# Two-block transformer kernel: the modulation products end with the attention, and three chunks of the first expert get homes

## The reference

```python
for l in range(DEPTH):                                    # 2 layers
    mod   = (silu(c)     @ ada_w[l] + ada_b[l])           # "modulation": ada_w[l] is 1024 x 6144
    mod_c = (silu(c_ctx) @ ada_w[l] + ada_b[l])
    sh1, sc1, g1, sh2, sc2, g2 = split(mod, 6)
    hx = rms_norm(x, norm1_g[l]) * (1 + sc1) + sh1        # and hc likewise for the context
    px = hx @ w_in[l]                                     # projection
    # four mixers on parts of px: spatial gating, fourier, attention "c" (differential), attention "d" (neighbourhood)
    x = x + g1 * (rms_norm(y, per head) @ w_out[l])       # merge
    h = rms_norm(x, norm2_g[l]) * (1 + sc2) + sh2
    aff = softmax(h @ router_w[l])                        # 16 experts, each takes its 32 best tokens of a stream
    x = x + g2 * sum over experts of gate * (silu(xe @ wg[e]) * (xe @ wu[e])) @ wd[e]
```

## Time and profile before

| | |
|---|---|
| median of 3 runs | 2338.39 us |
| lowest and highest run | 2334.14 and 2344.38 us |
| profiled execution, span from first to last instruction | 2346.5 us |
| PE busy, share of the span | 2140.5 us, 91% |
| DMA | 660.95 MB, mean 282 GB/s |
| layer 0 up to the first product of expert 0 | 0 to 323 us |
| layer 0's experts | 323 to 780 us |

### The profile page before, as it was taken

How to read it: one execution, slowest core, us unless ns; L and a number is a source line. 1 busy time by engine, 2 the same in 40 slices (tenths; PEclk the granted TensorE clock), 3 DMA queues, 4 the chain that set the end, 5 groups by cost and what they waited for, 6 DMA issues and landing times.

```text
span 2346.5 us, 33361 instructions
## 1 busy us (share of the span) xinstructions
PE 2140.5 (91%) x14368; PEld 1483.4 (63%) x14368; DVE 1132.2 (48%) x1775; ACT 844.9 (36%) x1258; POOL 44.2 (2%) x76
## 2 busy tenths in 40 slices
PE   9999999989898999966565789999999999999998
PEld 5866743423232777533232348888988888888887
DVE  5646531212121777310010138668877677568765
ACT  4436321111111556200000025445655455456544
POOL 0022000000000011000000000000000000000000
PEclk9999999999999999988888899999999999999999
DMA  8375679999999553999999994454554544364442
GB/s 347 120 318 246 257 310 425 427 427 428 428 427 426 201 224 140 377 427 426 428 427 427 426 407 182 149 210 171 189 190 159 195 180 180 135 234 180 157 172 88
DMA packets 66978, 660.95 MB, mean 282 GB/s; under 512 B 7504, under 2 KB 10576, under 8 KB 21136
## 3 DMA queue, kind: packets, MB, share of 16 engines
q1 hardware_dynamic: 66832, 658.83, 69.3%
HBM read 657.76 MB, written 1.05 MB: 281 GB/s over the span
## 4 chain that ended last, share of the span: by engine, by line
PE 69%; DMA 24%; DVE 3%; ACT 2%; issue 1%; SPq 0%; DVEq 0%; ACTq 0%
PE ps L967 21%; PE ps L1460 11%; PE ps L968 10%; DMA ring_top<-in_exp_up 9%; DMA ring_top<-in_exp_down 5%; PE ps L937 5%; PE ps L938 5%; PE ps L939 5%; DMA ring_top<-in_exp_gate 4%; DMA ring<-in_exp_up 3%; PE ps L986 2%; DMA ring<-in_exp_down 1%; DMA ring<-in_ada_w 1%; PE ps L1154 1%; PE ps L1453 1%; PE ps L1417 1%
## 5 line engine op out<-in xcount | busy, mean ns | idle before, releaser
L967 PE MATMUL ps<-h_buf_r,ring_r 128*128 128x512 f32 x800 | 283.8, 399 | 1.5 <-DVE h_buf_r L759 1.5
L1460 PE MATMUL ps<-ring,arena 128*32 128x256 f32 (+1 forms) x1632 | 215.0, 514 | 67.3 <-DMA ring<-in_exp_up 38.0
L2787 DVE TENSOR_TENSOR h_buf<-h_buf,ps 128x512 f32<-128x512 f32 (+1 forms) x32 | 17.8, 555 | 490.0 <-PE ps L1460 478.1
L968 PE MATMUL ps<-h_buf_r,ring_r 128*128 128x256 f32 x800 | 224.7, 281 | 0.0
L967 PE MATMUL ps<-h_buf_r,ring_top_r 128*128 128x512 f32 x608 | 217.4, 402 | 2.9 <-DVE h_buf_r L759 2.9
L1460 PE MATMUL ps<-ring_top,arena 128*32 128x256 f32 (+1 forms) x1328 | 164.2, 512 | 59.5 <-DMA ring_top<-in_exp_up 29.0
L1460 PEld LDWEIGHTS ps<-ring,arena 128*32 128x32 f32 (+1 forms) x1632 | 80.1, 132 | 199.0 <-issue 109.5
L485 DVE TENSOR_TENSOR ring_r<-ring,ring_r 128x2048 fp32r<-128x2048 f32 (+4 forms) x92 | 177.7, 1967 | 50.6 <-ACT ring_r L477 50.5
L967 PEld LDWEIGHTS ps<-h_buf_r,ring_r 128*128 128x128 f32 x800 | 150.3, 188 | 39.2 <-issue 1.9
L968 PE MATMUL ps<-h_buf_r,ring_top_r 128*128 128x256 f32 x608 | 171.4, 282 | 0.0
L1460 PEld LDWEIGHTS ps<-ring_top,arena 128*32 128x32 f32 (+1 forms) x1328 | 61.9, 133 | 159.1 <-issue 84.6
(11 more groups left out here) (390 smaller groups left out, 4144.7 us busy)
## 6 DMA issues: line engine op xcount, KB each, us to landing
ring<-in_exp_gate SPq DMA_DIRECT2D x35, 2048.0 KB, 28.2
ring<-in_exp_down SPq DMA_DIRECT2D x35, 2048.0 KB, 30.5
ring<-in_exp_up SPq DMA_DIRECT2D x34, 2048.0 KB, 30.2
ring_top<-in_exp_gate SPq DMA_DIRECT2D x29, 2048.0 KB, 29.1
ring<-in_ffn_w SPq DMA_DIRECT2D x50, 1024.0 KB, 6.9
ring_top<-in_exp_up SPq DMA_DIRECT2D x24, 2048.0 KB, 30.7
ring_top<-in_exp_down SPq DMA_DIRECT2D x24, 2048.0 KB, 28.3
ring_top<-in_ffn_w SPq DMA_DIRECT2D x38, 1024.0 KB, 6.9
```

Of the source, the lines that this page charges most:

```text
L967: release(pe.matmul(ps[:, bank, :], w[0][:, lo:lo + P], both, start=start, stop=False, skip_group_check=True))
L968: return pe.matmul(ps[:, bank, 0:N], w[1][:, lo:lo + P], both[:, 0:N], start=False, stop=stop, skip_group_check=True)
L1460: mm = pe.matmul(out, stationary, slot(c)[:, at:at + width], start=start, stop=stop)
```

## The change

Steps 1 and 2 of the modulation move into the projection: a pair of chunks behind each of the first four `w_in` chunks. Step 3 takes step 1's place ahead of the fourier mixer, steps 4 and 5 take the places of 3 and 4 among the units of attention d, and the block ahead of attention d and the four pieces in the route go away; in the route, products of zeros stand in their place. SP's list follows this order, so `w_in` and `ada_w` chunks alternate. At the start, the second half of step 0 is mixed with two products of the projection's second pair. The first expert's chunks c1, c2 and c3 get homes in `arena` (c2 had one already), the home of the modulation chunk goes, and a table of the experts (`aff_bc`) moves to make room. The squares for the second norm keep four tiles in turn instead of eight, since c3's home lies where the other four were. The core of the diff:

```diff
         HOMES = {
+            ("experts", 0, 1): [part(8192, 10240), part(14336, 16384)],
             ("experts", 0, 2): [part(10240, 14336)],
-            ("ada", 5, 3): [part(8192, 10240), part(14336, 16384)],
+            ("experts", 0, 3): [part(2048, 4096), part(6144, 8192)],
...
             if l == 0:
                 stream(("ada", 0), *[PLAIN] * 4)
-            stream(("w_in", l), HALVED, HALVED, HALVED, (2, SLOT), (1, KT * GROUP))
-            if l == 0:
-                for step in range(1, 5):
+                for c in range(4):
+                    stream(("w_in", 0, c), w_in_chunks[c])
+                    stream(("ada_pair", 1 + c // 2, c % 2), PLAIN, PLAIN)
+                stream(("w_in", 0, 4), w_in_chunks[4])
+                for step in range(3, 6):
                     stream(("ada", step), *[PLAIN] * 4)
...
+                        if l == 0 and (e, c) == (1, 0):
+                            sp.wait_ge(sem("d_pv"), len(units(0)))
+                            load_expert_home(0, 1)
+                            load_expert_home(0, 2)
+                            sp.wait_ge(sem("y_turned"), KT)
+                            load_expert_home(0, 3, (0,))
+                        if l == 0 and (e, c) == (1, 2):
+                            sp.wait_ge(sem("mix_out"), KT)
+                            load_expert_home(0, 3, (1,))
...
+                if i == 1 and k >= 4:
+                    act.wait_ge(sem("mix_square_added"), k - 3)
+                act.activation(square_of(i, k)[:, 0:width], x_res[:, k, 0:width], ACT.Square).then_inc(sem("norm_squares"), 1)
...
                     first_pair(0, range(0, 4))
-                    for c in range(2):
-                        first_ada_products(1, c)
-                    first_pair(1, range(0, 2))
+                    first_ada_products(1, 0)
+                    first_pair(1, (0,))
+                    first_ada_products(1, 1)
+                    first_pair(1, (1,))
                     first_ada_turn(1)
...
                     owed[0] += 1
+                    ada_products(1, (0, 1))
...
+                        if l == 0 and c in (1, 2, 3):
+                            ada_products(1 + c // 2, (2, 3) if c % 2 else (0, 1))
+                    elif l == 0 and t == 0 and c in (2, 4):
+                        ada_turn(c // 2)
...
                     pe.wait_ge(sem("c_out"), 4)
-                    ada_products(2)
...
-                        ada_products(3 + i // 4, (i % 4,))
+                        ada_products(4 + i // 4, (i % 4,))
...
                 if l == 0:
-                    ada_products(5, (0,))
+                    stay_busy(3, 8)
...
-                    ada_products(5, (1,))
+                    stay_busy(3, 6)
...
-                if l == 0:
-                    ada_products(5, (2,))
-                else:
-                    stay_busy(3, 2)
+                stay_busy(3, 2)
...
                 if l == 0:
-                    ada_products(1)
+                    ada_products(3)
```

More of the change, by code:

```diff
@@ L406, in build, with w_in, ada_chunk @@
             stream(("ple", l), HALVED, HALVED)
+        def w_in(l, c):
+            return chunk_at["w_in", l, c]
+        def ada_chunk(step, i):
+            return chunk_at["ada_pair", step, i // 2] + i % 2 if step in (1, 2) else chunk_at["ada", step] + i
         def expert_chunk(l, e):
@@ L572, in load_expert_home, with ada @@
                           P * SLOT * (2 * (EXPERTS * l + e) + which % 2), pieces)
[L574 to L578, removed]
-                    else:
[L580 to L584, removed]
+            def ada(step, pieces=range(4)):
+                for i in pieces:
+                    load(ada_chunk(step, i), "ada_w", SLOT)
             def ffn(i):
@@ L702, in squares, with square_of @@
                 part(2560, 4608).rearrange("p (k t) -> p k t", k=KT)
+        def square_of(i, k):
+            if i == 1:
+                return part(0, 2048).rearrange("p (k t) -> p k t", k=4)[:, k and 1 + (k - 1) % 3, :]
+            return squares(i)[:, k, :]
         def norm_pe(pe, release, i):
@@ L978, in ada_products @@
                     pe.wait_ge(sem("ada_mod"), step + 1)
[L979 to L987, removed]
+                for i in pieces:
+                    n = ada_chunk(step, i)
+                    chunk(n)
+                    for k in (2 * i, 2 * i + 1):
+                        for j in range(4):
+                            at = 2048 * (k % 2) + 512 * j
+                            mm = pe.matmul(ps[32 * j:32 * j + 32, 7, :], cond[:, k, :], slot(n)[:, at:at + 512],
+                                           start=k == 0, stop=k == KT - 1)
                             release(mm)
-                    if k % 2:
-                        mm.then_inc(weights_used, 1)
+                    mm.then_inc(weights_used, 1)
             def first_ada_products(half, c):
-                n = chunk_at["ada", 0] + 2 * half + c
+                n = ada_chunk(0, 2 * half + c)
                 if half == c == 0:
@@ L1029, in job_product @@
                     c, t, lo, width, _ = jobs[j]
-                    w = halves(base + c)
+                    w = halves(w_in(l, c))
                     own = slice(P * t, P * t + P)
@@ L1358, in token_means @@
                     own, out = slice(P * t, P * t + P), ps[:, 7, 64 + t:65 + t]
[L1359 to L1360 removed]
+                    release(pe.matmul(out, square_of(i, 0)[:, own], mean_col[:, :], start=True, stop=False))
+                    mm = pe.matmul(out, square_of(i, KT - 1)[:, own], mean_col[:, :], start=False, stop=True)
                 mm.then_inc(sem("norm_mean"), 1)
@@ L1503, in experts @@
                                 mm.then_inc(weights_used, 1)
-                            if l == e == which == 0 and k == 3:
-                                ada_turn(5)
                             if (which, k) != (1, KT - 1):
```

170 lines of the change are left out of this document (83 added, 87 removed).

## The result

The changed kernel takes 2345.3 us (median of 20 runs, 2342.5 to 2354.8) against 2341.5 us of the kernel before (20 runs): a ratio of 1.0026, with a 95% interval of 1.0017 to 1.0035, or +4 to +8 us. It is slower by less than the 0.5% that was set as the bound for "same"; 2343 us and "same" were forecast. The 2343 was reckoned from the 2338.4 us of three runs; what it says of the change is +4.6 us. The two medians differ by +3.9, and the ratio, which is not that of the medians, stands for +6 us.

A forecast was written before the change was run, and what follows sets the result against it. PE's progress to expert 0's chunk c4 was taken to start an unbroken DMA stream of 85 expert chunks. Terms 14.1 + 1.3 − 1.4 − 6.6 − 2.8 = +4.6 on 2338.4 gave 2343 us, range 2331 to 2355.

The forecast's parts named there:

- The homes at nothing: Layer 0's experts: homes for the first expert's c1 to c3 leave the start of the expert load stream unchanged, 0 us.
- The rival of two chunks ahead: Layer 0's experts: added homes shorten the load stream by 2 × 4.9 us, to 2333 us; chance 0.09.
- Projection, +14.1 + 1.3 − 1.4 = +14.0: Projection: two modulation steps add 14.1 us, their two turns 1.3, and a covered weight wait at the start saves 1.4.
- Attention d, −6.6: Attention d: without the block of step 2, the first value product starts 6.6 us earlier.
- The route with the turn, −2.8: Layer 0's route: four step 5 pieces replaced by zeros, and its turn inside expert 0 gone, save 2.8 us.
- Sum, +4.6: All terms up to PE finishing expert 0's chunk c4: 4.6 us later, with everything after moving along unchanged.
- Loads in the projection at nothing: Projection: the fifth `w_in` chunk, now among modulation loads, still lands in time with some 4 us free; 0 us.
- Low clock after the route: Start of expert 0: zeros fail to hold PE's clock, +4 to +9 us, 2347 to 2352; chance 0.06.
- Four tiles of squares at nothing: Merge, second norm: four tiles in place of eight cost nothing under PE's pace; +1.7 us without that cover.

The follow-up runs named there:

- homes used twice: Changed kernel with the places of c2 and parts of c3 and c1 reused for two later expert chunks; 2340.8 us, 0.9998 of the kernel before.
- the late chunk: Changed kernel with the fifth `w_in` chunk issued behind two more modulation chunks; 2352.9 us, 1.0060 of the kernel before.
- one step back: Changed kernel with only step 1 in the projection, step 2 ahead of the fourier mixer, step 3 ahead of attention d; 1.0027 of the kernel before.
- the two edits together: Changed kernel with the places of c2, c3 and c1 used a second time and no zeros in layer 0's route; 2336.3 us, 0.9985 of the kernel before.

## Why the prediction was right, point by point

**The homes at nothing:** right, and shown by undoing them (1.0023 against 1.0026). The rival of two chunks ahead fell with it. The Trainium skill's rule of early issue ("DMA: Bandwidth & Descriptors", "Rules for kernel authors") is not wrong here: the run that used the places a second time shows early loads worth 6.55 us at the end of the experts. What the rule names as gained is the fixed setup cost of a load; two whole chunks off the stream were the prediction's reading of it. But the homes as changed do not let anything go out earlier while DMA rests (share 0.23 from 335 to 350 us); a load can start only when a place is free.

**Projection, +14.1 + 1.3 − 1.4 = +14.0:** measured +14.25 from the start of the program, but +14.9 from the second half of step 0, where the changed kernel was 0.64 us ahead by chance (33.62 to 133.00 against 32.98 to 147.25). So the term was 0.9 us too small. The products are four times 3.57 us from a pair's first record to the next product (54.13 to 57.70), 14.3; the handover to and from the projection's products, which was not priced, adds about 0.2 us to each (57.70 to 58.04 behind the first pair, where two products in a row stand 0.23 apart). The wait of 1.42 us is gone, as taken. That the term is on the path was shown by leaving half of it out: 6.8 us at the projection's end, 6.5 at e1c5.

**Attention d, −6.6:** 7.45 − 14.25 = −6.8. **The route with the turn, −2.8:** 7.45 at attention d is 4.74 at expert 0, −2.7 already there, and 4.0 at e1c5, a further −0.8 with the turn; so the two together were undersized by some 0.7 us. Two of its parts differ: the transposes behind the first zeros stand at 315.37 and not at the 309.2 + 7.5 = 316.7 of a plain shift, a gain of 1.3 us where I took half of it. In that execution the eight zeros took 3.25 us. With homes used twice they took 3.57, the products ahead of them 0.8 us more, and expert 0 came 1.47 us later: where the clock falls there differs from run to run. The granted clock in the zeros' stretch was 0.56 in the changed kernel, 0.50 with the homes used twice, and 1.00 in the run with part of step 1 left out, where the eight took 1.89 us.

**Sum, +4.6:** +4.0 at e1c5 (351.02 against 347.37 − 0.33), or +4.6 counted from 33 us, +3.7 at the end of the experts, +3.9 between the medians, +4 to +8 us by the ratio. The path is the one forecast. That the number is so close is partly luck: the cost in the projection was put 0.9 us too low, the savings at attention d and in the route together 0.9 us too low as well, so that the two cancel, and the route alone varies by over 2 us from one execution to another. The rest of the program moved along unchanged up to 1690 us, where the shift is +3.9; behind that the two traces cannot show it.

**Loads in the projection at nothing:** right in the result, but the slack was overstated, about 2 us in place of 4. The step that failed is "ACT's halving of 1.90 and then its reads": between them ACT has 1.99 us of other work and a table load of 1.28, and the load landed in time only because the queue was short (5.8 us from issue to landing). And a loss there costs more than its wait: of the 11.0 us that the late chunk cost, 3 lay behind the wait, most of them at the low clock, which the price left out.

**Low clock after the route:** fell, since expert 0's first chunk takes 3.65 us with and without zeros.

**Four tiles of squares at nothing:** the shift is +7.45 us at attention d and +7.55 at the first product of the logits behind the merge (307.62 against 300.07), so at most 0.1 us was lost there. This was not tested by itself.

## What to carry to other kernels

When a stage is bound by a stream of loads, find the event that starts the unbroken stream, and ask of each edit whether it moves that event. Here more places filled ahead of it only lengthened the rest of the DMA before it; places that came free during that rest were worth time. And work that is moved to a stage where PE is fully busy costs its whole time there, while the old place gives back only what PE does not have to wait for anyway: here a step cost 7.8 us in the projection (the run with one step back), while attention d gave back 6.8 us for one step and the route with its turn 3.5 for the other.

## What was not expected

**Column blocks side by side.** Products that fill 32 columns of the array, at four places, overlap fully: 4 records took 1.90 us and 16 took 1.92. Leaving out columns saved nothing; leaving out every second row block brought the end of the projection 6.8 us forward.

**A slow stretch at the full clock.** The shift of +3.9 us holds to 1690 us and is +0.2 at 2020. In the profiled execution of before, the same products were 1.5% slower there, with the clock granted in full (1.00) and PE without a wait. First before, 1700 to 1870 us, then the changed kernel, 1703 to 1870, then the kernel of the two edits together, 1700 to 1870 (busy us, mean ns of one):

```profile
L967 PE MATMUL ps<-h_buf_r,ring_r 128*128 128x512 f32 x192 | 68.2, 400 | 0.0
```

```profile
L988 PE MATMUL ps<-h_buf_r,ring_r 128*128 128x512 f32 x192 | 66.9, 394 | 0.0
```

```profile
L998 PE MATMUL ps<-h_buf_r,ring_r 128*128 128x512 f32 x206 | 73.0, 399 | 0.0
```

The two levels, 394 and 399 to 400 ns, do not go with the change: in this stretch the kernel before and the last one shown lie at the upper level and the other eight traces at the lower, while from 1300 to 1690 us the changed kernel, too, lies at 399. So one execution's span says less about another's than landmarks do: this hid the 3.9 us. What sets the level in a stretch stays open.
